# The middle third of the adaLN modulation: from TensorE to row sums on VectorE

## The chip, the cores and the metric

One core of a Trainium2 chip runs the whole program. The metric is the device time of one execution in microseconds; lower is better. TensorE (PE) multiplies matrices, VectorE (DVE), ScalarE (ACT) and GpSimd (POOL) work on rows of 128 partitions, SyncE (SP) here only issues transfers. Every engine takes its own instructions in order; engines wait for one another on semaphores.

## What is computed

Two groups of 128 tokens (context and latent) go through two layers. Each layer begins its modulation from the condition, one row for each group, and uses the same weights for both:

```python
def _modulation(cond, w, b):
    m = jax.nn.silu(cond) @ w + b            # [1, 1024] @ [1024, 6144]
    return jnp.split(m[:, None, :], 6, axis=-1)

sh1, sc1, g1, sh2, sc2, g2 = _modulation(c, p['ada_w'], p['ada_b'])
mix = mixers(_modulate(x, p['norm1'], sh1, sc1), ...)   # three branches: MLA, RG-LRU, differential attention
x = x + g1 * mix
x = x + g2 * _moe(_modulate(x, p['norm2'], sh2, sc2), p)  # top 4 of 32 experts
```

Thirds of the 6144 outputs are made at three times: sh1 and sc1 before the first norm, g1 and sh2 (the middle third) in the middle, sc2 and g2 before the second norm. g1 is first needed when the mixers' output is added to x, sh2 at the second norm. All is float32.

## The kernel before

**Stages of a layer.** The front part: norm, modulation third 0, input projection (units u of `win_mm`), MLA projections, recurrent gates and scans, the merge with its gates, attention in 12 units (8 MLA heads, 4 differential heads), output projection, second norm, router. Then 13 expert passes or more, which stream the expert weights.

**Weights and the ring.** The front's weights stand in DRAM as 32 positions of up to 2 MB (`front`), and go through a ring of 6 slots in SBUF: position p lies in slot p % 6. SyncE issues them strictly in order of position (L416 to L420); each waits until the position 6 places before it has been used (`consumed`, L332). Positions 15 to 18 are the middle third of `ada_w`, 19 the branch-1 output weights, 20 and 21 the gates of branch 0, 23 its output weights, 22 and 24 the gates of branch 2, 25 to 28 the last third of `ada_w`. After position 31 come the first expert weights (L430), each when a slot is free.

**The middle third before.** `ada_products(1, 0)` on TensorE (L545): the SiLU of the condition (`cT`, 128 x 32 columns of which two are used) is the stationary side and the weights stream, 4 positions x 8 = 32 products (64 matmul records). Its output is copied by ScalarE (`modulation`, L1046), transposed back by TensorE (L554), and VectorE adds the bias into `modT` and makes `g1h` = g1/2 (L1201). It stands on TensorE between the eight gate products of branch 1 (`merge(8)`, L675) and the first output product (`merge(1)`, L679). `mod_rdy` 2 is awaited before the transposes of the first attention unit (L684).

**The merge.** A list MERGE of 56 products is worked off in order, its items placed between other work. Product f writes one of two PSUM halves, so it waits until product f - 2 has been evacuated (`merge_evac`, L351): gates by ScalarE (`merge_gates`, a Tanh, L1043), output products by VectorE (`merge`, L1415 to L1443). Products 0 to 7 are gates of branch 1 (positions 13 and 14), then output products and gates alternate from 8 on: 8 is the first output product, 9 the first gate of branch 0 (position 20), 24 the first output product of branch 0.

**Order on the engines around the change.** ScalarE: input projections evacuated up to `win_evac(13)` (L1027), a store, `merge_gates(8)`, `modulation(1, 0)`, then attention. VectorE: norms and rotations of the MLA heads, the scans of both directions (L1357 to L1389), the norms and rotations of the differential heads (L1392 to L1406), two operations on lambda (L1409, L1410), `modulation(1, 1)`, `merge(1)`, then in each attention unit: maxima (L1459), a copy, the probabilities (L1472 or L1480 to L1484, `pn_v`), one or two merge evacuations, and in units 8 to 11 the norm of the head's output (L1497 to L1507). TensorE in a unit: scores, the next unit's transposes, a gate product (two products from unit 8 on), the transposes of the probabilities, an output product, the product with the values.

Of the kernel before, what the change touches and what calls it, by code (L numbers as in the profile page):

```python
# [20 lines left out]
ALU = mybir.AluOpType  # L21
# [3 lines left out]
P = 128  # L25
D = 1024
# [101 lines left out]
    return len(range(s, PRE, RING)) - 1  # L128

def build(nc, x_in, cond_in, consts, vecs, rows, front, lru_gate_w, router_w, exp_w1, exp_b1, exp_w2, exp_b2,
          cache_ckv, cache_krope, cache_dk, cache_dv, y_out, new_ckv, new_krope, new_lru, new_dk, new_dv):
    ctx = ExitStack()
    with ctx:
        def sb(name, shape, dt=F32):
            return ctx.enter_context(nc.sbuf_tensor(name, shape, dt))
# [35 lines left out]
        ring = sb("ring", [P, RING, SLOT])  # L172
        arena = sb("arena", [P, 21344])
        meta = sb("meta", [P, 3], I32)
        both = sb("both", [P, MAX_EXTRA // 2], I32)
        ps = ctx.enter_context(nc.psum_tensor("ps", [P, 8, 512], F32))

        def at(off, *dims):
# [8 lines left out]
            if len(dims) == 4:  # L187
# [101 lines left out]
            [sem(f"{n}{i}") for i in range(2)] for n in ("nrm_mm", "nrm_sqrt", "hraw", "h_dve", "h_act"))  # L289
        ada_mm, ada_sb, ada_tr, prep, mod_rdy = (sem(n) for n in  # L290
                                                 ("ada_mm", "ada_sb", "ada_tr", "prep", "mod_rdy"))
        sp_abs, sp_ln, lam_exp = sem("sp_abs"), sem("sp_ln"), sem("lam_exp")
        win_mm, win_v, win_a = sem("win_mm"), sem("win_evac_v"), sem("win_evac_a")
        mla_n, conv_rdy = sem("mla_norm"), sem("conv_rdy")
# [37 lines left out]
        def consumed(pos):  # L332

            for r in range(3):
                if S_ADA[r] <= pos < S_ADA[r] + 4:
                    return ada_mm, r + 1
            if pos in S_IN:
                return win_mm, 2 * (S_IN.index(pos) + 1)
            if pos in (S_QB, S_KVB):
                return p4_mm, {S_QB: 4, S_KVB: 10}[pos]  # L340
            return f_mm, max(f for f, m in enumerate(MERGE) if merge_slot(*m) == pos) + 1

        def arrived(eng, pos):
# [67 lines left out]
        with nc.Fori(0, L) as l:  # L411
            with nc.Block() as block:
# [120 lines left out]
                def _(pe):  # L533
# [11 lines left out]
                    def ada_products(r, bank):  # L545

                        slots = [arrived(pe, S_ADA[r] + j) for j in range(4)]
                        for k in range(KC):
                            for j in range(4):
                                last = mm(ps[32 * j:32 * j + 32, bank, :], cT[:, k, :],  # L550
                                          slots[j][:, k * 512:(k + 1) * 512], start=k == 0, stop=k == KC - 1)
                        last.then_inc(ada_mm, 1)

                    def ada_transposes(r, bank):  # L554
                        pe.wait_ge(ada_sb, r + 1)
                        for b in range(4):
                            last = tr(ps[:, bank, b * P:(b + 1) * P], msb[r][:, b * P:(b + 1) * P], ident)
                        last.then_inc(ada_tr, 1)
# [115 lines left out]
                    pe.wait_ge(p3_ev, 5)  # L674
                    merge(8)  # L675
                    pe.wait_ge(win_a, 8)
                    ada_products(1, 0)
                    ada_transposes(1, 1)
                    merge(1)  # L679

                    def qk_transposes(u):
                        if u == 0:
                            pe.wait_ge(mod_rdy, 2)  # L684
                            pe.wait_ge(qn_rdy, 2)
# [226 lines left out]
                def _(act):  # L912
# [80 lines left out]

                    act.wait_ge(prep, 2)
                    A(lam[:, 4:6], lam[:, 0:2], ACT.Exp).then_inc(lam_exp, 1)
                    for u in (6, 7):
                        win_evac(u)
                    for v in range(10):
# [26 lines left out]
                    lru_roots(1)  # L1025
                    win_evac(12)
                    win_evac(13)  # L1027
                    act.wait_ge(win_a, 7)
                    store(new_dv, projd[:, 2, 0, :])

# [13 lines left out]
                              scale=0.5).then_inc(f_ac, 1)  # L1044

                    def modulation(r, bank):  # L1046
                        act.wait_ge(ada_mm, r + 1)
                        A(msb[r], ps[:, bank, :], ACT.Copy).then_inc(ada_sb, 1)

                    merge_gates(8)  # L1050
                    modulation(1, 0)
                    act.wait_ge(lru_rdy, 1)
                    store(new_lru, fin[:, :])
                    act.wait_ge(dn_rdy, 3)
# [91 lines left out]
                def _(dve):  # L1146
# [53 lines left out]

                    def modulation(r, bank):  # L1201

                        dve.wait_ge(ada_tr, r + 1)
                        src = ps[:, bank, :].rearrange("p (b j z) -> p j b z", b=4, j=4)[:, :, :, 0:G]
                        dst = modT[:, 16 * r:16 * r + 16, :].rearrange("p (j b) z -> p j b z", j=4)
                        bias = vec[:, V_ADAB + 16 * r:V_ADAB + 16 * r + 16].rearrange("p (j b) -> p j b", j=4)
                        link(V.tensor_tensor(dst, src, bias[:, :, :, None].broadcast_to((P, 4, 4, G)), ALU.add))
                        if r == 1:
                            V.tensor_scalar(g1h[:, :, :], modT[:, 16:24, :], 0.5, None, ALU.mult).then_inc(mod_rdy, 1)
                        else:  # L1210
                            out, sc, nrm = ((A1, 8, V_N1), None, (A2, 32, V_N2))[r]
                            V.scalar_tensor_tensor(out=out[:, :, :], in0=modT[:, sc:sc + 8, :], scalar=1.0,
                                                   in1=vec[:, nrm:nrm + 8][:, :, None].broadcast_to((P, KC, G)),
                                                   op0=ALU.add, op1=ALU.mult).then_inc(mod_rdy, 1)

                    dve.wait_ge(ada_mm, 1)
                    V.tensor_copy(msb[0], ps[:, 0, :]).then_inc(ada_sb, 1)
# [224 lines left out]
                                                                  op0=ALU.mult, op1=ALU.add)  # L1442
                                last.then_inc(f_dv, 1)  # L1443

                    modulation(1, 1)
                    dve.wait_ge(mod_rdy, 2)
                    merge(1)

                    def qk_copy(u):
# [5 lines left out]
                    for u in range(12):  # L1455
# [18 lines left out]
                        else:  # L1474
# [8 lines left out]
                            for n, c in enumerate((slice(0, 128), slice(128, 384))):  # L1483
                                last = V.scalar_tensor_tensor(out=probs[j][:, 0, c], in0=probs[j][:, 1, c],  # L1484
                                                              scalar=nl[:, n:n + 1], in1=probs[j][:, 0, c],
                                                              op0=ALU.mult, op1=ALU.add)
                        last.then_inc(pn_v, 1)
                        if u != 7:
                            merge(1 if u < 7 else 2)
                        if u < 8 and u % 2:  # L1490
# [2 lines left out]
                        if u >= 8:  # L1493
                            dve.wait_ge(pv_mm, u + 1)
                            if u > 8:
                                dve.wait_ge(ot_mm, u - 8)
                            link(V.tensor_copy(on[:, :, :], ps[:, 5, 0:NT].rearrange("p (g n) -> p g n", g=G)))  # L1497
                            for g in range(G):
                                last = V.tensor_tensor_reduce(out=onsq[:, g, :], in0=on[:, g, :],
                                                              in1=on[:, g, :], scale=1.0, scalar=0.0, op0=ALU.mult,  # L1500
                                                              op1=ALU.add, accum_out=ss[:, g:g + 1])
                            link(last)
                            link(V.tensor_scalar(ss[:, 0:2], ss[:, 0:2], 1.0 / DV, EPS, ALU.mult, ALU.add))
                            rsqrt(ss[:, 0:2])
                            for g in range(G):
                                last = V.tensor_scalar(on[:, g, :], on[:, g, :], ss[:, g:g + 1], None, ALU.mult)
                            last.then_inc(on_v, 1)  # L1507
                    merge(8)
                    modulation(2, 1)
                    merge(8)  # L1510
# [293 lines left out]
```

## Time and profile before

| | |
|---|---|
| median of 3 runs | 1724.07 us (1723.03 to 1724.40) |
| the profiled execution | 1722.77 us, its span 1721.1 us |
| TensorE busy | 1529.2 us (89% of the span) |
| VectorE, ScalarE, GpSimd busy | 565.4, 258.1, 3.8 us |
| transfers | 545.86 MB, mean 317 GB/s |
| granted TensorE clock, mean | 0.946 of full |

How the rows are read. A row of the timeline gives the start in us from the span's start, the length in us, the engine, the line, the operation, what it writes <- what it reads, with shapes where the engine has them, and how many instructions are merged into it (x64); in brackets stands how long the engine was idle before it and what ended that.
### The profile page before, as it was taken

The numbers are of one execution on the slowest core, as the hardware profiler recorded it, in microseconds if no ns is written. First come the engines' busy times: TensorE is split into PE (matmuls) and PEld (weight loads), VectorE is DVE, ScalarE is ACT, GpSimd is POOL, SyncE is SP. The second block draws the span as 40 slices with busy tenths as digits, with TensorE's granted clock in tenths as the row PEclk, the third lists the DMA queues.
The fourth block names the chain that finished last, engine by engine and source line by source line (L and its number), as shares of the span: only waits on it lengthen the run. The fifth ranks groups of instructions, "written<-read, shape, count | busy, mean of one in ns | idle before, by whom it ended". The sixth has DMA issues, their size and how long they took to land. (4 is left out here: it accounts for less than half of the span.)

```text
span 1721.1 us, 20139 instructions
## 1 busy us (share of the span) xinstructions
PE 1529.2 (89%) x8000; PEld 891.9 (52%) x8000; DVE 565.4 (33%) x1443; ACT 258.1 (15%) x579; POOL 3.8 (0%) x6
## 2 busy tenths in 40 slices
PE   4999999989889989595969999999897997996868
PEld 2756788764444444242438477878553543442424
DVE  2368236353611121111133862452615121111112
ACT  2034122030000000000030432220200000000001
POOL 0000000000000000000000000000000000000000
PEclk8999999999989999798989999999998999998979
DMA  9653622938999999999895346338489999999991
GB/s 373 260 199 137 267 110 87 390 154 341 419 432 409 411 430 432 430 429 432 345 368 214 150 153 251 147 133 361 176 347 420 430 408 423 430 430 431 431 419 75
DMA packets 48710, 545.86 MB, mean 317 GB/s; under 512 B 12704, under 2 KB 13472, under 8 KB 15584
## 3 DMA queue, kind: packets, MB, share of 16 engines
q1 hardware_dynamic: 39488, 539.95, 75.6%
q10 hardware_dynamic: 9120, 4.53, 1.0%
q8 instruction: 66, 1.08, 0.2%
q14 instruction: 36, 0.29, 0.0%
HBM read 542.06 MB, written 2.40 MB: 316 GB/s over the span
## 5 line engine op out<-in xcount | busy, mean ns | idle before, releaser
L858 PE MATMUL ps<-ring,arena 128*64 128x512 f32 (+2 forms) x1632 | 373.1, 641 | 62.8 <-DMA ring<-exp_w_dram 36.1
L858 PEld LDWEIGHTS ps<-ring,arena 128*64 128x64 f32 (+2 forms) x1632 | 115.5, 133 | 281.7 <-issue 280.2
L878 PE MATMUL ps<-ring,arena 128*32 128x512 f32 (+2 forms) x768 | 199.6, 662 | 28.3 <-DMA arena<-exp_w_dram 16.3
L858 PE MATMUL ps<-arena 128*32 128x512 f32 (+1 forms) x480 | 189.7, 660 | 9.1 <-DMA ring<-exp_w_dram 9.1
L671 PE MATMUL ps<-hT,ring 128*128 128x256 f32 x768 | 171.4, 379 | 0.0
L671 PEld LDWEIGHTS ps<-hT,ring 128*128 128x128 f32 x768 | 144.1, 190 | 19.4 <-issue 1.0
L878 PE MATMUL ps<-arena 128*64 128x512 f32 (+1 forms) x288 | 124.0, 651 | 26.8 <-DMA ring<-exp_w_dram 26.8
L671 PE MATMUL ps<-arena,ring 128*128 128x256 f32 x640 | 144.6, 380 | 2.9 <-ACT arena L1064 1.6
L671 PEld LDWEIGHTS ps<-arena,ring 128*128 128x128 f32 x640 | 118.8, 190 | 19.0 <-issue 2.7
L632 PE MATMUL ps<-ring,hT 128*128 128x512 f32 (+1 forms) x320 | 119.7, 534 | 1.9 <-DVE hT L1227 1.9
L819 PEld LDWEIGHTS ps<-arena 128*128 128x128 f32 x896 | 107.6, 197 | 24.9 <-issue 19.0
L819 PE MATMUL ps<-arena 128*128 128x128 f32 x896 | 114.8, 283 | 3.9 <-DVE arena L1553 3.9
L1126 ACT ACTIVATE arena<-arena 128x512 f32<-128x512 f32 x26 | 16.4, 630 | 668.8 <-DVE arena L1662 668.8
L878 PEld LDWEIGHTS ps<-ring,arena 128*32 128x32 f32 (+2 forms) x768 | 58.6, 136 | 100.8 <-issue 100.8
L1560 DVE TENSOR_TENSOR arena<-arena 128x256 f32<-128x256 f32 x26 | 11.0, 425 | 282.9 <-PE ps L858 282.8
L1674 DVE COPY arena<-ps 128x512 f32<-128x512 f32 x26 | 18.0, 692 | 241.4 <-PE ps L878 241.4
L886 PE MATMUL ps<-arena 128*128 128x256 f32 x416 | 96.5, 385 | 0.0
L886 PEld LDWEIGHTS ps<-arena 128*128 128x128 f32 x416 | 77.1, 190 | 30.1 <-issue 20.6
L632 PEld LDWEIGHTS ps<-ring,hT 128*128 128x128 f32 x320 | 57.4, 190 | 62.7 <-issue 61.5
L1662 DVE TENSOR_SCALAR arena<-ps 128x512 f32<-128x512 f32 x26 | 18.0, 691 | 190.6 <-PE ps L858 190.6
L858 PEld LDWEIGHTS ps<-arena 128*32 128x32 f32 (+1 forms) x480 | 50.3, 134 | 54.3 <-issue 54.3
L878 PEld LDWEIGHTS ps<-arena 128*64 128x64 f32 (+1 forms) x288 | 33.0, 134 | 74.5 <-issue 74.5
(282 smaller groups left out, 1377.7 us busy)
## 6 DMA issues: line engine op xcount, KB each, us to landing
ring<-exp_w_dram SPq DMA_DIRECT2D x148, 2048.0 KB, 18.7
ring<-front_dram SPq DMA_DIRECT2D x58, 2048.0 KB, 8.8
arena<-exp_w_dram SPq DMA_DIRECT2D x47, 2048.0 KB, 19.4
ring<-front_dram SPq DMA_DIRECT2D x2, 1152.0 KB, 16.2
ring<-front_dram SPq DMA_DIRECT2D x2, 1024.0 KB, 18.2
ring<-front_dram SPq DMA_DIRECT2D x2, 640.0 KB, 27.2
xT<-x_in_dram SPq DMA_DIRECT2D x1, 1024.0 KB, 4.9
arena<-lru_gate_w_dram ACTq DMA_DIRECT2D x4, 256.0 KB, 6.4
```

Of the source, the lines that this page charges most:

```text
L632: last = mm(ps[:, bank, 0:w], hT[:, k, half * P:(half + 1) * P], slot[:, k, :], start=k == 0, stop=k == KC - 1)
L671: last = mm(out, slot[:, k, cols], src[:, k, :], start=k == 0, stop=k == nk - 1)
L819: last = mm(ps[:, 2 + k // 4, (k % 4) * P:(k % 4 + 1) * P], X2[:, g, k * P:(k + 1) * P], S_s[:, g, :], start=g == 0, stop=g == 1)
L858: last = mm(ps[c, h, :], xTg[:, 4 * part + k, c], w[i][:, k, h * 512:(h + 1) * 512], start=False, stop=True, skip_group_check=True)
L878: last = mm(ps[c, 2 + h, :], actT[:, f, c], w[i][:, f, h * 512:(h + 1) * 512], start=f == 0, stop=f == 3)
L886: last = mm(ps[:, 4 + k // 2, (k % 2) * NT:(k % 2 + 1) * NT], O_s[:, k * P:(k + 1) * P], SCT[:, :], start=first and k % 2 == 0, stop=True, ...
L1126: A(sig_s, gate_s, ACT.Sigmoid, scale=ALPHA).then_inc(sig_a, 1)
L1560: V.tensor_tensor(SC_s.rearrange("p g (i w) -> p g i w", i=n), S_s.rearrange("p g (i w) -> p g i w", i=n), cwT[:, :, cols][:, :, :, None]. ...
L1662: V.tensor_scalar(gate_s, ps[:, 0, :], LIMIT, None, ALU.min).then_inc(gate_v, 1)
L1674: V.tensor_copy(O_s[:, 512:1024], ps[:, 3, :]).then_inc(o_v, 1)
```

## The change

The weights of the middle third are laid out with the output features on the partitions: a position holds four blocks of 128 features, each with all 1024 inputs in a row. The condition comes a second time as one row of 2 x 1024 numbers and is copied to all 128 partitions (`cB`, 1 MB written, issued by ScalarE). ScalarE makes its Tanh into one scratch tile (`cjunk`), VectorE multiplies, group by group: cB = (tanh(c/2) + 1) * c, twice the SiLU. Then VectorE makes 32 row sums a layer, one for each block and group: 0.5 * sum(weights * cB) straight into `modT`. Four stand before the first merge evacuation, three in each of units 0 to 7 behind the probabilities, four in unit 8. `middle_modulation` adds the bias and makes `g1h` after unit 11. TensorE's products and transposes of this third, ScalarE's copy and the wait for `mod_rdy` 2 on TensorE go. The ring slots of positions 15 to 18 are now freed by every eighth row sum (`ada_v`). The counts of `ada_mm`, `ada_sb` and `ada_tr` are renumbered.

```diff
@@ consumed()
             for r in range(3):
                 if S_ADA[r] <= pos < S_ADA[r] + 4:
-                    return ada_mm, r + 1
+                    return (ada_v, pos - S_ADA[r] + 1) if r == 1 else (ada_mm, r // 2 + 1)
@@ TensorE
                     merge(8)
                     pe.wait_ge(win_a, 8)
-                    ada_products(1, 0)
-                    ada_transposes(1, 1)
                     merge(1)
...
                         if u == 0:
-                            pe.wait_ge(mod_rdy, 2)
                             pe.wait_ge(qn_rdy, 2)
@@ ScalarE
                     A(lam[:, 4:6], lam[:, 0:2], ACT.Exp).then_inc(lam_exp, 1)
+                    act.dma_start(cB[:, :, :].rearrange("p g n -> p (g n)"), cond_rows.broadcast_to((P, G * D))).then_inc(
+                        ld_cb, 16)
...
                     win_evac(12)
                     win_evac(13)
+                    act.wait_ge(ld_cb, 16)
+                    for g in range(G):
+                        if g:
+                            act.wait_ge(cb_prod, g)
+                        A(cjunk[:, :], cB[:, g, :], ACT.Tanh, scale=0.5).then_inc(cb_tanh, 1)
                     act.wait_ge(win_a, 7)
                     store(new_dv, projd[:, 2, 0, :])
...
                     merge_gates(8)
-                    modulation(1, 0)
@@ VectorE
+                    dots = [0]
+
+                    def modulation_dots(n):
+
+                        for _ in range(n):
+                            i, g = dots[0] // G, dots[0] % G
+                            dots[0] += 1
+                            if i % 4 == 0 and g == 0:
+                                arrived(dve, S_ADA[1] + i // 4)
+                            slot = ring[:, (S_ADA[1] + i // 4) % RING, :].rearrange("p (c k) -> p c k", k=D)
+                            last = V.tensor_tensor_reduce(out=cjunk[:, :], in0=slot[:, i % 4, :], in1=cB[:, g, :],
+                                                          scale=0.5, scalar=0.0, op0=ALU.mult, op1=ALU.add,
+                                                          accum_out=modT[:, 16 + i, g:g + 1])
+                            if i % 4 == 3 and g == 1:
+                                last.then_inc(ada_v, 1)
+                                dve.wait_ge(ada_v, i // 4 + 1)
+                            else:
+                                link(last)
+
+                    def middle_modulation():
+
+                        dve.wait_ge(ada_v, 4)
+                        link(V.tensor_tensor(modT[:, 16:32, :], modT[:, 16:32, :],
+                                             vec[:, V_ADAB + 16:V_ADAB + 32][:, :, None].broadcast_to((P, 16, G)),
+                                             ALU.add))
+                        V.tensor_scalar(g1h[:, :, :], modT[:, 16:24, :], 0.5, None, ALU.mult).then_inc(mod_rdy, 1)
...
-                    modulation(1, 1)
-                    dve.wait_ge(mod_rdy, 2)
+                    for g in range(G):
+                        dve.wait_ge(cb_tanh, g + 1)
+                        V.scalar_tensor_tensor(out=cB[:, g, :], in0=cjunk[:, :], scalar=1.0, in1=cB[:, g, :],
+                                               op0=ALU.add, op1=ALU.mult).then_inc(cb_prod, 1)
+                    dve.wait_ge(cb_prod, 2)
+                    modulation_dots(4)
                     merge(1)
...
                         last.then_inc(pn_v, 1)
+                        modulation_dots(3 if u < 8 else 4 if u == 8 else 0)
                         if u != 7:
                             merge(1 if u < 7 else 2)
...
+                    middle_modulation()
+                    dve.wait_ge(mod_rdy, 2)
                     merge(8)
                     modulation(2, 1)
```

## Rows read from the trace of the kernel before

**Rows 1.** The page's busy times, us (share of the span) xinstructions.
```profile
PE 1529.2 (89%) x8000; PEld 891.9 (52%) x8000; DVE 565.4 (33%) x1443; ACT 258.1 (15%) x579; POOL 3.8 (0%) x6
```
**Rows 2.** Timeline of TensorE: gate products, the removed block, what follows; then layer 1.
```profile
153.43 27.79 PE L671 MATMUL ps<-hT,ring 128*128 128x256 f32 x128
181.15 7.07 PE L550 MATMUL ps<-ring,cT 128*32 128x512 f32 x64
...
189.43 1.89 PE L671 MATMUL ps<-arena,ring 128*128 128x256 f32 x8
...
193.67 3.62 PE L671 MATMUL ps<-hT,ring 128*128 128x256 f32 x16
...
1031.82 7.07 PE L550 MATMUL ps<-ring,cT 128*32 128x512 f32 x64
```
**Rows 3.** Windows: the attention units 8 to 11.
```profile
253.00:304.80 51.80, 51.80 (x282) 44.21 (x281) 32.42 (x135) 13.64 (x49) 0.00 (x0) 1.00 0.34 135
```
**Rows 4.** Timeline of SyncE's queue: the first expert weights of layer 0.
```profile
312.66 1.76 SPq L430 DMA_DIRECT2D ring<-exp_w_dram  x3
```
**Rows 5.** Timeline of VectorE: its chain before the removed block; then layer 1.
```profile
155.55 1.22 DVE L1389 TENSOR_TENSOR arena<-arena 128x1024 f32<-128x1024 f32 x1
...
176.33 0.16 DVE L1410 TENSOR_TENSOR lam<-lam,vec 128x1 f32<-128x1 f32 x1
189.70 0.19 DVE L1207 TENSOR_TENSOR modT<-ps,vec 128x32 f32<-128x32 f32 x1 [13.21 <-PE ps L557]
...
1026.99 0.16 DVE L1410 TENSOR_TENSOR lam<-lam,vec 128x1 f32<-128x1 f32 x1
```
**Rows 6.** Timeline of ScalarE: win_evac(13) and the first gate.
```profile
153.63 0.60 ACT L968 ACTIVATE arena<-ps 128x512 f32<-128x512 f32 x1 [2.73 <-PE ps L632]
...
157.08 0.47 ACT L1043 ACTIVATE arena<-ps,bmh 128x256 f32<-128x256 f32 x1 [1.56 <-PE ps L671]
```
**Rows 7.** Timeline of ScalarE: one operation over 2048 and one over 512 elements.
```profile
5.64 1.91 ACT L394 ACTIVATE arena<-xT 128x2048 f32<-128x2048 f32 x1 [3.63 <-DMA xT<-x_in_dram]
...
147.51 0.63 ACT L992 ACTIVATE arena<-arena 128x512 f32<-128x512 f32 x1
```
**Rows 8.** Timeline of TensorE after waits of several lengths; windows behind the first.
```profile
27.26 9.59 PE L550 MATMUL ps<-ring,cT 128*32 128x512 f32 x64 [13.14 <-DMA ring<-front_dram]
...
456.92 7.07 PE L858 MATMUL ps<-ring,arena 128*32 128x512 f32 x64 [3.26 <-DMA ring<-exp_w_dram]
...
1309.39 8.53 PE L858 MATMUL ps<-ring,arena 128*32 128x512 f32 x64 [3.37 <-DMA ring<-exp_w_dram]
...
28.10:30.60 2.50, 2.50 (x16) 0.67 (x12) 2.47 (x6) 1.28 (x2) 0.00 (x0) 0.50 0.99 419
...
32.80:36.80 4.00, 4.00 (x40) 1.09 (x32) 0.40 (x2) 0.00 (x0) 0.00 (x0) 1.00 1.14 323
```
**Rows 9.** One line's instructions: the 20 ring loads of 60 to 330 us.
```profile
DMA to landing us min/median/max: 7.0/7.7/22.2
```
**Rows 10.** Timeline of VectorE: two row sums of squares (L1240, L1244).
```profile
58.00 0.56 DVE L1240 CUSTOM_DVE_ANT_0 arena<-arena 128x384 f32<-128x384 f32 x1
...
58.48 0.42 DVE L1244 CUSTOM_DVE_ANT_0 arena<-arena 128x256 f32<-128x256 f32 x1
```
**Rows 11.** Timeline of VectorE in attention units 1 and 2.
```profile
201.03 0.29 DVE L1459 TENSOR_REDUCE nm<-ps 128x1 f32<-128x128 f32 x1 [1.23 <-PE ps L723]
...
202.84 0.55 DVE L1472 TENSOR_SCALAR arena<-arena,rcp 128x128 f32<-128x128 f32 x2
207.09 0.42 DVE L1426 SCALAR_TENSOR_TENSOR arena<-arena,ps 128x256 f32<-128x256 f32 x1 [3.71 <-PE ps L671]
...
208.74 0.29 DVE L1459 TENSOR_REDUCE nm<-ps 128x1 f32<-128x128 f32 x1 [0.43 <-PE ps L723]
```
**Rows 12.** Timelines of VectorE and TensorE in attention unit 8.
```profile
258.39 0.41 DVE L1431 SCALAR_TENSOR_TENSOR arena<-arena,ps 128x256 f32<-128x256 f32 x1
...
259.98 1.89 PE L671 MATMUL ps<-arena,ring 128*128 128x256 f32 x8
```

More of the change, by code:

```diff
@@ L128, in later_uses, with build @@
     return len(range(s, PRE, RING)) - 1
-def build(nc, x_in, cond_in, consts, vecs, rows, front, lru_gate_w, router_w, exp_w1, exp_b1, exp_w2, exp_b2,
+def build(nc, x_in, cond_in, cond_rows, consts, vecs, rows, front, lru_gate_w, router_w, exp_w1, exp_b1, exp_w2, exp_b2,
           cache_ckv, cache_krope, cache_dk, cache_dv, y_out, new_ckv, new_krope, new_lru, new_dk, new_dv):
@@ L174, in build @@
         meta = sb("meta", [P, 3], I32)
+        cB = sb("cB", [P, G, D])
+        cjunk = sb("cjunk", [P, D])
         both = sb("both", [P, MAX_EXTRA // 2], I32)
@@ L291, in build @@
                                                  ("ada_mm", "ada_sb", "ada_tr", "prep", "mod_rdy"))
+        ld_cb, cb_tanh, cb_prod, ada_v = sem("cond_rows_in"), sem("cond_tanh"), sem("cond_silu"), sem("ada_dve")
         sp_abs, sp_ln, lam_exp = sem("sp_abs"), sem("sp_ln"), sem("lam_exp")
@@ L554, in ada_transposes @@
                     def ada_transposes(r, bank):
-                        pe.wait_ge(ada_sb, r + 1)
+                        pe.wait_ge(ada_sb, r // 2 + 1)
                         for b in range(4):
@@ L1046, in modulation @@
                     def modulation(r, bank):
-                        act.wait_ge(ada_mm, r + 1)
+                        act.wait_ge(ada_mm, r // 2 + 1)
                         A(msb[r], ps[:, bank, :], ACT.Copy).then_inc(ada_sb, 1)
                     merge_gates(8)
-                    modulation(1, 0)
                     act.wait_ge(lru_rdy, 1)
@@ L1201, in modulation @@
                     def modulation(r, bank):
-                        dve.wait_ge(ada_tr, r + 1)
+                        dve.wait_ge(ada_tr, r // 2 + 1)
                         src = ps[:, bank, :].rearrange("p (b j z) -> p j b z", b=4, j=4)[:, :, :, 0:G]
@@ L1207, in modulation @@
                         link(V.tensor_tensor(dst, src, bias[:, :, :, None].broadcast_to((P, 4, 4, G)), ALU.add))
[L1208 to L1214, printed above, removed]
+                        out, sc, nrm = ((A1, 8, V_N1), None, (A2, 32, V_N2))[r]
@@ new lines, in modulation @@
+                        V.scalar_tensor_tensor(out=out[:, :, :], in0=modT[:, sc:sc + 8, :], scalar=1.0,
+                                               in1=vec[:, nrm:nrm + 8][:, :, None].broadcast_to((P, KC, G)),
+                                               op0=ALU.add, op1=ALU.mult).then_inc(mod_rdy, 1)
+                    dots = [0]
[14 more added lines that the diff above has]
+                                link(last)
@@ L1763 @@
         for j in range(4):
-            front[S_ADA[r] + j] = blocks(a["ada_w"], (4 * r + j) * 512, 512)
+            c0 = (4 * r + j) * 512
+            if r == 1:
+                front[S_ADA[r] + j] = a["ada_w"][:, :, c0:c0 + 512].transpose(0, 2, 1).reshape(
+                    L, 4, P, D).transpose(0, 2, 1, 3).reshape(L, P, -1)
+            else:
+                front[S_ADA[r] + j] = blocks(a["ada_w"], c0, 512)
     for p, (c0, n) in zip(S_IN, IN_SLICES):
@@ L1776 @@
         "cond_in": cond.T.reshape(KC, P, G).transpose(1, 0, 2),
-        "consts": constants(np), "vecs": vecs, "rows": rows,
+        "cond_rows": cond.reshape(1, -1), "consts": constants(np), "vecs": vecs, "rows": rows,
         "front": np.concatenate(front, axis=2),
@@ L1789 @@
             "new_dk": (L, P, 512), "new_dv": (L, P, 512)}
-    nc = _bacc.Bacc("TRN2", target_bir_lowering=False, num_devices=1)
+    nc = _bacc.Bacc("TRN2", target_bir_lowering=False, num_devices=1, dynamic_dma_scratch_size=1024)
     given, args = {}, []
```

## The prediction

> **What bounds the kernel now.** I read the page first: TensorE is busy 89% of the span, VectorE 33%, ScalarE 15% [rows 1]. That is a mean over two different halves of each layer (front, then experts), so next I read the timeline by engine around the operations that the change touches, in layer 0. Layer 1 repeats it: there the block that the change removes begins 1031.82 - 1026.99 = 4.83 us after VectorE's last operation of its chain, in layer 0 181.15 - 176.33 = 4.82 us [rows 2, 5]. Between 153.43 and 181.15 us TensorE runs the eight gate products of branch 1 with no gap (3.46 us each), then the 64 matmuls of the second modulation (7.07 us), a short wait, four transposes and the first product of the merge at 189.43 [rows 2]. The attention that follows is TensorE's as well: 51.80 of 51.80 us busy in its second part [rows 3]. So TensorE is the bound of the front part, and what is taken from or added to its chain counts in full. The front's end sets the expert part too: the transfers of expert weights are issued only from 312.66 us on, since each waits for a ring slot that the front's last products free [rows 4]. Nothing there can run ahead, so a front that is late by x makes the layer late by x.
>
> **Removed from TensorE.** The block of ada_products(1) and ada_transposes(1) with its copy on ScalarE and its two operations on VectorE runs from 181.15 to 189.43 us: -8.28 us per layer [rows 2]. VectorE then was idle 13.21 us before it had this to do [rows 5], so its own removal is worth nothing.
>
> **Added on ScalarE, and its wait.** This is where I expect the time to go. The new order on ScalarE is win_evac(13), Tanh of group 0, a wait for cb_prod 1, Tanh of group 1, and only then merge_gates(8). cb_prod 1 comes from VectorE's product for group 0, which the change puts where modulation(1,1) stood: behind the scans, the four squares, the norms and the rotations of the differential heads and behind L1410. In the trace that chain is dense from 154 us to L1410 at 176.33 + 0.16 = 176.49 us [rows 5], while ScalarE is free from 154.2 us and makes its first gate at 157.08 [rows 6]. So queued behind ScalarE's wait are all eight gates, and TensorE waits for them: there are two PSUM halves for the merge, so product 2 needs gate 0 evacuated. It began at 153.43 + 2 x 3.455 = 160.34 us. Now: VectorE's product over 128x1024 takes 1.22 us (as L1389 [rows 5]), 176.53 to 177.78. ScalarE's Tanh over 1024 elements is in no row; 512 take 0.63 and 2048 take 1.91 [rows 7], so 0.83 ns an element in between and 1.06 us, to 178.87; the gate of 0.47 us overlaps it by 0.1 and ends at 179.25. TensorE goes on at 179.3: a stall of **18.96 us** per layer. The first Tanh (154.2 to 156.6 with the table load of 1.28 us that moves there) is hidden, as is the product of group 1 (to 180.2) and the first four sums (to 185.4), since VectorE's next duty, the first merge, is not due before TensorE has made six more gates (20.8 us).
>
> After long waits TensorE is slow: the 64 matmuls of L550 take 9.59 us after 13.14 us idle [rows 8] and 7.07 us where they follow other work [rows 2]; behind the wait the granted clock is 0.50, the lower level of 1.2 GHz, and from 32.8 us on 1.00 [rows 8]. I add +2.2 us (bounds 1.5, as 64 matmuls of the experts with 8.53 us for 7.07 [rows 8], and 2.5).
>
> **The slot of position 20.** Its ring slot (2) is freed by gate product 7, the last before the removed block, and it holds the first gates of branch 0, product 9. Before, 181.15 to 193.67 = 12.5 us lay between; without the block it is 193.67 - 189.43 = 4.24 us [rows 2]. A 2 MB load takes 7.0 us at least from issue to landing and 7.7 in the median [rows 9]; alone on the queue I take 7.0. So the removed block was the cover of this load, and **+2.8 us** come back (up to 3.5). The Trainium skill has a price for it ("DMA: Bandwidth & Descriptors", section on what a DMA costs: about 2.0 us plus the bytes by 436 GB/s), which would be 6.8 us and a stall of 2.6 us; the row is used.
>
> **The sums of products on VectorE.** 32 per layer, over 1024 elements, each linked to the next. The same operation over 384 elements takes 0.56 us, over 256 0.42 [rows 10], so 1.09 ns an element; for 1024 that is 1.26 us, and I take 1.27 with the link (1.2 to 1.5). In units 0 to 7 three of them, 3.81 us, go between the probabilities (203.39) and the merge's operation at 207.09, where VectorE is idle 3.71 us [rows 11]: 0.1 us late. The merge's result is needed by TensorE only in the next unit and the next maximum is due at 208.74 [rows 11]; with 0.44 and 0.42 us for the two operations in between, up to (208.74 - 203.39 - 0.86) / 3 = 1.50 us each are hidden. Cost 0. Unit 8 has four, 5.08 us, and no such gap: there the merge follows the probabilities at once at 258.39, and TensorE starts product 26 at 259.98, which needs product 24 evacuated [rows 12]. Now the sums run 258.39 to 263.47, the two operations of the evacuation to 264.33, and product 26 starts at 264.38: **+4.4 us** (4.1 to 5.3). VectorE's long chain after it (norm of the head) shifts equally, and later units have no idle time that could give it back [rows 3].
>
> **Positions 21 to 24** are freed by sums 8, 16, 24 and 32 instead of all at 188 us. 21 and 22 have several units to land. A unit takes 208.74 - 201.03 = 7.71 us [rows 11]; 23 is issued with the second sum of unit 6 at 203.39 + 5 x 7.71 + 2.5 = 244.4 us, lands by 252.1 and is needed in unit 8, which begins at 253: hidden by a microsecond or two. 24 is issued in unit 8 with 25 to 27 queued behind it on SyncE (some 20 us of transfer); it is needed in unit 10 and they after unit 11, some 45 us on: nothing. The load of the condition (1 MB, written to all partitions) goes out on ScalarE's queue near 43 us and is wanted at 154: nothing; the ring's loads that it shares the engines with have 9 us of reserve. middle_modulation is 0.5 us on VectorE while TensorE makes the third modulation: hidden.
>
> **Clock after the two short waits.** After waits of 3.26 and 3.37 us the next 64 matmuls took 7.07 and 8.53 us [rows 8]: 0 to 1.5 us more. I take 0.8 for each of the two, **+1.6 us**. The Trainium skill ("TensorE: Matmul & The Clock Gate", section "HAM oscillation") says that a wait for data of this size puts the array back to the lower clock each time. By it each would cost the full 2.2 us and the kernel 5.6 us more in all.
>
> **Sum.** Per layer -8.28 + 18.96 + 2.2 + 2.8 + 4.4 + 1.6 = +21.7 us, two layers +43.4. On the profiled execution's 1722.77 us (span 1721.1 and 1.67 around it) that is 1766.2; the runs' median of 1724.07 lies 1.3 above it. I predict 1766.5 us.
>
> **Rivals.**
> (A) ScalarE is not held, because cb_prod 1 can come before VectorE's chain is over, so not slower: -8.28 + 2.8 + 4.4 + 1.6 = +0.5 per layer, 1724 us. For it: the operation needs nothing of that chain. Against it: it stands behind it in the one order of VectorE, which shows no gap in the chain. It decides as soon as cb_prod 1 comes before 157 us. Chance 0.03.
> (B) Only the hold counts; position 20 lands in time and the sums of unit 8 delay nothing: 2 x (18.96 + 2.2 - 8.28) = +25.8, 1748.6 us. For it: loads were never waited for in this stage. Against it: 4.24 against 7.0 us, and 5.08 us of sums ahead of an evacuation with 0.7 us of slack. Chance 0.12 (for either of the two vanishing, 1752 to 1760).
> (C) The sums are slower than their small relatives. From 1.57 us on, VectorE's unit (3.2 us + three sums) is longer than TensorE's 7.71 and becomes the bound: at 1.7 us 8 x 0.39 less the 1.4 us of slack = 1.7 us per layer and 1.7 more in unit 8: 1773 us. Chance 0.08.
> (D) The lower clock after each wait, as the rule above has it: 1772 us. Chance 0.12.
> (E) The change does nothing of this, because the compiler or the queues order the operations otherwise: 1724. Below 0.02, no row speaks for it.
> My own case has the rest, 0.64.
>
> **Range.** Its low end is all clock costs at 0 and 1.2 us sums (+17.6 per layer, 1758), and case B with one term gone at 1752; the high end is 2.5, 3.5, 4.4 and 3.0 (+24.1 per layer, 1771), and C to 1773. I give 1753 to 1775. A measurement of this kernel tells about 0.2% (3.4 us) from no change. Slower 0.96, within 0.02, faster 0.02.
>
> **What will show it.** In the changed kernel: ScalarE idle some 20 us between two Tanh of 128x1024, released by VectorE; TensorE idle 19 us at the third gate product with ScalarE as the releaser, and the lower clock behind it; 2.8 us before product 9, released by a DMA; 32 sums near 1.26 us a layer; 4.4 us in unit 8 before product 26, released by VectorE. No gap in units 1 to 7. What would prove me wrong: the first gate at 157 us as before (A), or gaps in every unit (C).

## The result, and the profile after

The changed kernel takes 1775.16 us in the median of 4 runs (1774.53 to 1777.90) against 1724.24 us before: a ratio of 1.0302, 95% interval 1.0288 to 1.0317. It is slower by 51 us. I had forecast +43 (1766.5 us) and a range up to 1775.0; the direction and the three places were right, and the size fell just outside.

The profiled execution has a span of 1773.9 us. First the busy times of its page, to be read against [rows 1]: TensorE has 136 records fewer (2 x 68) and is yet busy 5.4 us longer, since other products became slower; VectorE has 82 us more, of which 78.3 us are the 64 row sums (1223 ns each).

```profile
PE 1534.6 (87%) x7864; PEld 898.5 (51%) x7864; DVE 647.4 (36%) x1575; ACT 260.8 (15%) x581; POOL 3.8 (0%) x6
```
```profile
L1229 DVE CUSTOM_DVE_ANT_0 cjunk<-ring,cB 128x1024 f32<-128x1024 f32 x64 | 78.3, 1223 | 1.6
```

The places are in TensorE's timeline of layer 0, which answers to [rows 2, 12]. Brackets: idle time before the row and what ended it.

```profile
152.40 7.07 PE L674 MATMUL ps<-hT,ring 128*128 128x256 f32 x32
178.21 23.95 PE L674 MATMUL ps<-hT,ring 128*128 128x256 f32 x96 [18.74 <-ACT arena L1050]
201.99 1.89 PE L674 MATMUL ps<-arena,ring 128*128 128x256 f32 x8
...
209.84 6.22 PE L674 MATMUL ps<-hT,ring 128*128 128x256 f32 x16 [3.46 <-DMA ring<-front_dram]
...
278.43 0.49 PE L742 MATMUL ps<-cst,arena 128*128 128x128 f32 x3
283.15 3.68 PE L674 MATMUL ps<-arena,ring 128*128 128x256 f32 x8 [4.24 <-DVE arena L1463]
```

Three waits stand there that before had none: 18.74 us before gate product 2, released by ScalarE; 3.46 us before product 9, released by a transfer; 4.24 us before product 26, released by VectorE. Behind each the products are longer: six gates in 23.95 us where eight took 27.79, so 3.1 us too long; product 9 in 6.22 for 3.62; product 26 in 3.68 for 1.89.

What holds ScalarE is in its timeline, which answers to [rows 6]: two Tanh of 1024 elements, with 21.17 us between them that end with VectorE's product (L1477), and only then the gates.

```profile
154.51 1.06 ACT L1034 ACTIVATE cjunk<-cB 128x1024 f32<-128x1024 f32 x1
176.73 1.06 ACT L1034 ACTIVATE cjunk<-cB 128x1024 f32<-128x1024 f32 x1 [21.17 <-DVE cB L1477]
...
177.70 0.82 ACT L1050 ACTIVATE arena<-ps,bmh 128x256 f32<-128x256 f32 x2
```

VectorE in unit 8: the last of the four sums, then at once the evacuation for which product 26 waits. Before, that evacuation began with the end of the probabilities [rows 12].

```profile
277.16 1.22 DVE L1229 CUSTOM_DVE_ANT_0 cjunk<-ring,cB 128x1024 f32<-128x1024 f32 x1
...
280.95 1.22 DVE L1229 CUSTOM_DVE_ANT_0 cjunk<-ring,cB 128x1024 f32<-128x1024 f32 x1
282.11 0.08 DVE L1229 DVE_READ_ACCUMULATOR2_ANT modT<- 128x1 f32 x1
282.22 0.42 DVE L1461 SCALAR_TENSOR_TENSOR arena<-arena,ps 128x256 f32<-128x256 f32 x1
```

Last, the windows of the changed kernel around the three waits; the third figure from the right is the granted clock.

```profile
171.10:178.20 7.10, 0.00 (x0) 0.00 (x0) 5.70 (x11) 1.47 (x3) 0.00 (x0) 0.50 0.08 30
...
181.00:184.00 3.00, 3.00 (x9) 2.37 (x8) 2.93 (x5) 0.00 (x0) 0.00 (x0) 0.50 0.00 0
184.00:187.00 3.00, 3.00 (x15) 2.64 (x14) 0.11 (x2) 0.48 (x1) 0.00 (x0) 0.96 0.00 0
206.40:209.80 3.40, 0.00 (x0) 0.00 (x0) 2.81 (x8) 1.18 (x5) 0.00 (x0) 0.75 0.92 360
...
212.00:214.00 2.00, 2.00 (x6) 1.55 (x6) 0.00 (x0) 0.00 (x0) 0.00 (x0) 0.50 0.00 0
...
278.90:283.10 4.20, 0.02 (x1) 0.00 (x0) 4.06 (x8) 0.00 (x0) 0.00 (x0) 1.00 0.00 0
283.10:285.00 1.90, 1.84 (x5) 1.49 (x6) 0.00 (x0) 0.85 (x2) 0.00 (x0) 0.53 0.93 276
```

Behind all three the clock is at its lower level, 0.50 (1.2 GHz), behind the short ones as well. At the first two it fell while TensorE was still idle (0.50 and 0.75 in the idle stretches); at the third the idle stretch still has 1.00 and the products behind it 0.53.

**The account.** From the first gate product to the router's products (L786) layer 0 takes 388.03 - 152.40 = 235.63 us; before it was 363.06 - 153.43 = 209.63. That is +26.0, layer 1 has +26.15. The parts for layer 0: 18.74 + 3.1 - 8.28 = +13.6 up to the first output product; 3.46 + 2.60 and some 0.15 = +6.2 at product 9; 4.24 + 1.79 and some 0.15 = +6.2 in unit 8 (in these rows a product begins 0.15 us before the end of the one before it where no wait parts them, and a wait takes that away too). The remaining 52.8 - 52.15 = 0.6 us of the span lie in the start and the experts.

### The profile page after: what moved, and what is told of

Read it like the earlier page. It is cut to its first block and busy times, and to the rows that moved or that the text cites. A ratio compares the mean times of both kernels' runs of the same rounds, so it can differ in the third digit from the quotient of the medians.

```text
span 1773.9 us, 20021 instructions
## 1 busy us (share of the span) xinstructions
PE 1534.6 (87%) x7864; PEld 898.5 (51%) x7864; DVE 647.4 (36%) x1575; ACT 260.8 (15%) x581; POOL 3.8 (0%) x6
## 5 line engine op out<-in xcount | busy, mean ns | idle before, releaser
L674 PE MATMUL ps<-hT,ring 128*128 128x256 f32 x768 | 182.9, 396 | 44.8 <-ACT arena L1050 37.5
L674 PEld LDWEIGHTS ps<-hT,ring 128*128 128x128 f32 x768 | 151.6, 200 | 68.5 <-ACT arena L1050 38.3
L1229 DVE CUSTOM_DVE_ANT_0 cjunk<-ring,cB 128x1024 f32<-128x1024 f32 x64 | 78.3, 1223 | 1.6
```

Of the source, the lines that this page charges most:

```text
L674: last = mm(out, slot[:, k, cols], src[:, k, :], start=k == 0, stop=k == nk - 1)
L1229: last = V.tensor_tensor_reduce(out=cjunk[:, :], in0=slot[:, i % 4, :], in1=cB[:, g, :], scale=0.5, scalar=0.0, op0=ALU.mult, op1=ALU.add, ...
```

## The experiments

**1. ScalarE not held.** The Tanh of group 1 writes a free part of the arena instead of the scratch tile, and waits for the scans only.

```diff
-                        if g:
-                            act.wait_ge(cb_prod, g)
-                        A(cjunk[:, :], cB[:, g, :], ACT.Tanh, scale=0.5).then_inc(cb_tanh, 1)
+                        if g:
+                            act.wait_ge(lru_fr, 2)
+                        A((cjunk[:, :], at(E0, D))[g], cB[:, g, :], ACT.Tanh, scale=0.5).then_inc(cb_tanh, 1)
...
+                    act.wait_ge(cb_prod, 2)
                     qk_copy(0)
```

> The changed kernel, but the Tanh of group 1 goes into a free part of the arena, so ScalarE doesn't wait for VectorE's chain and the gates go on at once. Theory (the hold costs its wait of 18.74 us and 3.15 us of lower clock behind it, per layer, and the other terms stay): 1775.2 - 2 x 21.9 = 1731.4 us, with TensorE still waiting 3.5 to 3.8 us for position 20 and 4.2 us in unit 8. Rival (the clock price behind the short waits comes from the long one before them): these 64 and 32 matmuls run at full clock, 2 x 2.6 us less, about 1726 us. Rival (the four sums, now due right when the first merge is, delay the first scores): 1 to 2 us more per layer, 1734.

Measured: 1731.78 us, ratio 1.0058 (1.0037 to 1.0080) to the kernel before. That is the time of my theory within 0.4 us: the hold with the lower clock behind it is 43 of the 51 us. The timeline of TensorE in layer 0 (first three rows) and layer 1 (last row) has the eight gates in one piece again, and the other two waits:

```profile
152.98 27.79 PE L674 MATMUL ps<-hT,ring 128*128 128x256 f32 x128
...
184.48 0.49 PE L722 MATMUL ps<-arena 96*128 96x128 f32 x2 [1.44 <-DVE arena L1487]
...
188.41 5.31 PE L674 MATMUL ps<-hT,ring 128*128 128x256 f32 x16 [2.46 <-DMA ring<-front_dram]
...
1043.60 6.08 PE L674 MATMUL ps<-hT,ring 128*128 128x256 f32 x16 [3.91 <-DMA ring<-front_dram]
```

The four sums delay the first scores by 0.9 us (1.44 for 0.52). In layer 0 the wait for position 20 is shorter by as much; in layer 1 it is 3.91 us all the same. Product 9 is slow in both (5.31 and 6.08 us) though no long wait precedes it, so the first rival falls.

**2. Eight sums first.** The four sums of unit 8 move before the attention.

```diff
-                    modulation_dots(4)
+                    modulation_dots(8)
...
-                        modulation_dots(3 if u < 8 else 4 if u == 8 else 0)
+                        modulation_dots(3 if u < 8 else 0)
```

> The changed kernel with the four row sums of unit 8 made before the attention (eight there, none in unit 8). Theory (unit 8 costs 4.24 us of wait and 1.8 us of lower clock per layer): 1775.2 - 2 x 6.0 = 1763.2 us, no wait of TensorE for VectorE in unit 8, and the eight sums hidden in VectorE's 19.9 us of idle time. Rival (the wait only moves to the next evacuation, since VectorE's norm of the head follows at once): under 2 us gained, 1773.

Measured: 1763.53 us, ratio 1.0237 (1.0220 to 1.0254), and no wait for VectorE in unit 8. Four sums at the wrong place cost 11.6 us in the two layers, a little more than their own 2 x 5.08 us, since the lower clock comes on top of the wait. Product 26 of layer 0 follows without a wait, at its old length:

```profile
280.93 0.49 PE L742 MATMUL ps<-cst,arena 128*128 128x128 f32 x3
281.26 1.89 PE L674 MATMUL ps<-arena,ring 128*128 128x256 f32 x8
```

**3. The hold alone, in the kernel before.**

```diff
+                    V.tensor_copy(krs[:, 3:4], lam[:, 7:8]).then_inc(hold, 1)     # VectorE, behind L1410
...
+                    act.wait_ge(hold, 1)                                          # ScalarE
                     merge_gates(8)
```

> The kernel before, with nothing but ScalarE's wait: the eight gates wait for a small VectorE operation behind L1410. Theory (the hold alone costs 18.7 us of wait and 3.15 us of lower clock): 1724.2 + 2 x 21.9 = 1768.0 us, and no wait for position 20, which the second modulation still covers. Rival (the clock price is that of my forecast, 2.2 us): 1766. Rival (part of the hold is absorbed, since VectorE and the loads run ahead meanwhile): under 1760.

Measured: 1763.04 us, ratio 1.0230 (1.0213 to 1.0247), 5 us under what I wrote. The wait is 16.73 us, not 18.74: this kernel has neither VectorE's product (1.23 us) nor the second Tanh (1.06 us) between the chain and the gates, which I had forgotten in the expectation. With 2.1 to 2.5 us of slow products behind it, 2 x 19.0 = 38 us on 1723.5 gives 1761.5. The waits of layer 0 and 1:

```profile
179.42 22.93 PE L672 MATMUL ps<-hT,ring 128*128 128x256 f32 x96 [16.73 <-ACT arena L1044]
...
1049.12 23.27 PE L672 MATMUL ps<-hT,ring 128*128 128x256 f32 x96 [16.73 <-ACT arena L1044]
```

The six gates take 22.93 and 23.27 us for 20.8, so behind a wait of 16.7 us the lower clock costs 2.1 and 2.4 us. On this term the first rival was right, and not the 3.15 us that I had taken over from the changed kernel: the price of a long wait is not one number. No wait for position 20 follows: the second modulation, still there, covers it.

**4. The block left out of the kernel before.** The products, copy and transposes of the middle third are left out, and the bias alone stands in modT, so this kernel does less than the reference; the weights are still loaded, and TensorE still waits for their arrival.

```diff
-                    merge(8)
+                    merge(7)
+                    for j in range(4):
+                        arrived(pe, S_ADA[1] + j)
+                    merge(1)
                     pe.wait_ge(win_a, 8)
-                    ada_products(1, 0)
-                    ada_transposes(1, 1)
```

> The kernel before without the middle third: its products, copy and transposes are left out and modT's third is the bias alone; its weights are still loaded and awaited. Theory (the block also covered the load of position 20): per layer -8.28 + 3.5 of wait + 2.5 of lower clock = -2.3, 1719.6 us, with a wait for a DMA before product 9. Rival (the block is worth its whole 8.28 us): 1707.7 us and no wait.

Measured: 1718.99 us, ratio 0.9977 (0.9965 to 0.9990), as the theory had it to 0.6 us. (The expert part of layer 1 gets other data here, so tenths are not to be read from it.) Even with nothing in its place the removed block is worth 4.5 us, not 16.6, since the load that it covered comes to light at once:

```profile
186.04 0.46 PE L722 MATMUL ps<-arena 96*128 96x128 f32 x2 [0.52 <-DVE arena L1452]
...
191.32 6.47 PE L671 MATMUL ps<-hT,ring 128*128 128x256 f32 x16 [3.84 <-DMA ring<-front_dram]
```

**5. Both mends, 1 and 2, together.**

> Both edits of the first two experiments: ScalarE not held, and eight sums before the attention, none in unit 8. Theory: the gain of unit 8 stays (2 x 6.0 us from 1731.8), but VectorE's idle time before the first merge is gone too, since TensorE is there 22 us earlier: chain to 175.5, two products and eight sums to 188.1, so the first scores come 6 us late; 3.5 of these lie under the wait for position 20, 2.5 don't: 1731.8 - 2 x 3.5 = 1724.8 us. Rival (sums before the attention are free): 1719.8.

Measured: 1725.99 us, ratio 1.0012 (1.0001 to 1.0023). The theory is off by 1.2 us. TensorE waits 6.50 us for the first transposes' copy, and behind it the granted clock is low again, 0.50 (the window below): product 9 takes 5.48 us though it has no wait of its own.

```profile
189.98 0.80 PE L722 MATMUL ps<-arena 96*128 96x128 f32 x2 [6.50 <-DVE arena L1487]
...
192.49 5.48 PE L674 MATMUL ps<-hT,ring 128*128 128x256 f32 x16
```
```profile
192.00:194.00 2.00, 2.00 (x8) 1.71 (x7) 1.54 (x6) 1.18 (x5) 0.00 (x0) 0.50 0.98 418
```

So sums before the attention are free only as long as TensorE is late itself.

**6. Early sums.** Both Tanh and both products near 70 to 81 us, four sums between the scan directions, four behind L1410, none in unit 8.

```diff
+                    act.wait_ge(ld_cb, 16)                 # ScalarE, ahead of win_evac(6)
+                    for g in range(G):
+                        A((cjunk[:, :], at(0, D))[g], cB[:, g, :], ACT.Tanh, scale=0.5).then_inc(cb_tanh, 1)
...
                         last.then_inc(lru_fr, 1)           # VectorE, in the loop over scan directions
+                        if d == 0:
+                            modulation_dots(4)
...
-                        modulation_dots(3 if u < 8 else 4 if u == 8 else 0)
+                        modulation_dots(3 if u < 8 else 0)
```

> The Tanh and the products with the condition made near 70 to 81 us, where ScalarE and VectorE are idle; four sums between the two scan directions, in VectorE's idle 6.2 us, four behind L1410, three in each of units 0 to 7, none in unit 8. Theory: all that is left of the change's costs is the wait for position 20 with its lower clock, per layer -8.28 + 3.6 + 2.5 = -2.2 us: 1719.1 us. Rival (a sum delays the recurrent chain or the ScalarE work behind it): a gap of TensorE elsewhere, 1722 or more.

Measured: 1718.42 us, ratio 0.9978 (0.9969 to 0.9988). The same time as without the whole computation (experiment 4): the 64 sums are hidden, and what is left is position 20. The timelines say it more sharply than the times: from gates to router this kernel takes 206.04 and 206.61 us in the two layers against 209.64 before, and 208.12 and 208.20 in experiment 4, and the 2 us between the two kernels in layer 0 are a shorter wait (3.16 us) with a cheaper low clock (1.5 us) before product 9:

```profile
190.84 5.08 PE L674 MATMUL ps<-hT,ring 128*128 128x256 f32 x16 [3.16 <-DMA ring<-front_dram]
```

So the front saves 3.6 and 3.0 us a layer where the theory had 2.2; that the whole time still came out as written is in part luck: 2.2 us are lost ahead of the first gate product (at 155.66 us for 153.43) and 2.4 us between the last router and the end (509.8 us for 507.4).

**7 and 8. Two or three output products ahead of the first gate of branch 0.** On top of 6 the merge list is shifted, so that more of TensorE's work lies between the issue of position 20 and its first use.

```diff
-for _b, _next in ((1, 0), (0, 2)):
-    for _ch in range(KC):
-        MERGE += [("proj", _b, _ch), ("gate", _next, _ch)]
+LEAD = 3                                                  # 2 in experiment 7
+MERGE += [("proj", 1, _ch) for _ch in range(LEAD)]
+for _ch in range(KC):
+    MERGE += [("gate", 0, _ch)] + ([("proj", 1, _ch + LEAD)] if _ch + LEAD < KC else [])
+for _ch in range(KC):
+    MERGE += [("proj", 0, _ch), ("gate", 2, _ch)]
```

> As the kernel with early sums, and two output products of branch 1 instead of one before the first gate of branch 0 (the merge list is shifted by one; unit 6 has no output product left). It gives the load of position 20 1.73 us more cover. Theory: the wait falls from 3.6 to 1.9 us, and behind so short a wait no lower clock; unit 6 without its output product costs 0.6 us, as unit 7 does: per layer -8.28 + 1.9 + 0.6 = -5.8, 1712 us. Rival (the lower clock comes after every wait): 1716.

Measured: 1715.93 us, ratio 0.9959 (0.9945 to 0.9973). The rival is right: the waits are 3.05 us in layer 0 and 1.86 us in layer 1, and behind even the shorter one the product takes 5.17 us for 3.62.

```profile
1037.87 5.17 PE L677 MATMUL ps<-hT,ring 128*128 128x256 f32 x16 [1.86 <-DMA ring<-front_dram]
```

> As before with three output products ahead: cover 4.24 + 3.46 = 7.7 us against a load of 7.2 to 7.8. Theory: no wait, no lower clock, 1.2 us for units 5 and 6 without their output product: per layer -8.28 + 0.1 + 1.2 = -7.0, 1709.5 us. Rival (the three evacuations on VectorE delay the first scores): 1 us more per layer.

Measured: 1712.14 us, ratio 0.9937 (0.9921 to 0.9954): 0.6% faster than the kernel before, beyond the interval, and the best version. No wait for a transfer is left in this stage; the rows of layer 0 show the gate of unit 0 at almost its full rate and a 0.62 us wait in one of the units without its output product.

```profile
188.72 3.69 PE L677 MATMUL ps<-hT,ring 128*128 128x256 f32 x16
...
231.91 0.43 PE L759 MATMUL ps<-arena 128*64 128x128 f32 x2 [0.62 <-ACT arena L1092]
```

From gates to router it saves 6.90 and 6.94 us in the two layers, 13.8 as expected; the span is only 10.7 shorter. In the last experts 3.4 us are lost again (510.8 us from the router's products to the end, 507.4 before), and 0.3 us are gained elsewhere. In the other kernels of this study with the same experts that stretch is 505.8 to 510.3 us, so one profiled execution doesn't tell whether the new order has a part in it. Why it differs is open.

**9. The waits filled.** The disputed term is what comes behind a wait. Here TensorE makes products that nobody reads instead of idling, in the changed kernel.

```diff
+                            if f == 2:
+                                pe.wait_ge(lg_ev, 16)
+                                fill(84)
+                            if f == 9:
+                                fill(14)
+                            if f == 26:
+                                pe.wait_ge(om_ev, 4)
+                                fill(18)
                             if f >= 2:
                                 merge_evac(pe, f)
```

> The changed kernel with every new wait of TensorE filled by products nobody reads: 84 of 128x256 before gate product 2 (18.1 of the 18.7 us), 14 before product 9 (3.0 of 3.5), 18 before product 26 (3.9 of 4.2). The waits themselves stay as long; only the idling goes. Theory (behind each wait the next products are slow because TensorE idled, 3.15 + 2.5 + 1.75 us per layer): the six gates take 20.8 us, product 9 3.6, product 26 1.9, and the kernel 1775.2 - 2 x 7.4 = 1760.4 us. Rival (the products behind the waits are slow for another reason, data or PSUM late): 1775 as before.

Measured: 1805.06 us, ratio 1.0473 (1.0456 to 1.0491). I had counted matmul records for products: the fills took twice the time and overran the waits. The experiment says little by its time, but the six gates behind took 20.88 us. So it was made again:

> As the kernel with the filled waits, with half the products: a float32 product of 128x256 is two matmul records and takes 0.432 us, so 84, 14 and 18 of them took 36.3, 6.0 and 7.8 us and overran the waits. 42, 7 and 9 take 18.1, 3.0 and 3.9 us and fit. Theory (the lower clock comes from the idling): the products behind the waits at full clock, 1775.2 - 2 x 7.4 = 1760.4 us. Rival (they are slow for another reason): 1775.

Measured: 1756.94 us, ratio 1.0213 (1.0185 to 1.0241); on the 1724.24 of the changed kernel's comparison that ratio is 1760.9 us, as the theory has it. The waits end at the same events, and the products behind them are back at their full rate:

```profile
160.00 18.29 PE L653 MATMUL ps<-hT,cst 128*128 128x256 f32 x84
178.88 20.99 PE L686 MATMUL ps<-hT,ring 128*128 128x256 f32 x96 [0.59 <-ACT arena L1062]
...
203.94 3.19 PE L653 MATMUL ps<-hT,cst 128*128 128x256 f32 x14
207.38 3.69 PE L686 MATMUL ps<-hT,ring 128*128 128x256 f32 x16 [0.26 <-DMA ring<-front_dram]
...
273.77 4.05 PE L653 MATMUL ps<-hT,cst 128*128 128x256 f32 x18
278.18 1.99 PE L686 MATMUL ps<-arena,ring 128*128 128x256 f32 x8 [0.35 <-DVE arena L1475]
```
```profile
206.00:212.00 6.00, 5.74 (x29) 4.75 (x28) 3.55 (x6) 0.85 (x2) 0.00 (x0) 1.00 0.22 85
```

The same stretch that had a granted clock of 0.50 to 0.75 has 1.00. More work on TensorE made the kernel some 15 us faster (10 to 19 us by the interval of the filled kernel): the slow products come from the idling, and not from late data or PSUM, whose waits are still there.

**10. The new order alone, in the kernel before.** The merge list of experiment 8, with the second modulation where it was.

> The kernel before with the new order of the merge alone: three output products of branch 1 ahead of the first gate of branch 0, none in units 5 and 6. Theory: nothing to win there, since the second modulation covers the load; 0.6 us more in each of units 5 and 6: 1723 + 2.5 = 1725.5 us. Then the gain of the best version comes from the block that left TensorE. Rival (the order itself is better): under 1720.

Measured: 1723.99 us, ratio 1.0005 (0.9995 to 1.0015). It gives nothing by itself; the 11 us of the best version are the removed block, once its cover is replaced.

## Why the prediction was right or wrong

**The direction and the places were right.** All three waits are where the sum had them, with the releasers that it named.

**The block removed, -8.28 us:** right. Experiment 4 shows it with its counterpart.

**ScalarE's hold, 18.96 us:** right, 18.74 in both layers. The Tanh that no row showed took 1.06 us, as interpolated.

**Position 20, 2.8 us:** right in kind, a bit small: 3.46 and 3.84. I took the fastest landing of [rows 9] for a load that has the queue to itself; the median, 7.7 us, would have given 3.5. In the kernel before this load did land in 7.0 us. In the changed one it took 7.4 and 7.8 us in the two layers, and within the same 4 us ScalarE issued two stores (256 KB and 4 KB), so it was not alone; no run took them away. The 6.8 us by the Trainium skill ("DMA: Bandwidth & Descriptors", section "Anatomy of one DMA — SWDGE (gpsimd) path") are worked from a fit that the page gives for transfers issued by GpSimd, while SyncE issues this one; that estimate is 0.6 us below the 7.4 us of layer 0.

**Row sums:** right. 1.22 us each and 1.27 from one to the next; hidden in units 0 to 7, where TensorE has no new wait, and 4.24 us in unit 8 for a forecast 4.4.

**The expert part:** right here. What the front lost came out at the end, to 0.6 us. In experiments 6 and 8 the last experts alone took 2.4 and 3.4 us longer than before, with no change to them.

**The lower clock behind the waits was the step that failed.** It had 2.2 us behind the long wait and 0.8 behind each short one, 3.8 us per layer. Measured are 3.1, 2.6 and 1.8 in layer 0, together 7.5, and 3.1, 2.4 and 1.7 in layer 1, together 7.3. The difference of 3.7 and 3.5 us is 7.2 us of the 9.4 us by which the forecast of the span was short (52.8 us for 43.4); the rest is position 20 (0.7 and 1.0 us) and 0.6 us outside the front parts. The 0.8 was a mean of two rows from expert passes, one of them without any loss [rows 8]. But the kernel before also had a 3.56 us wait in the same front part, before the router's products, whose windows I had read and not used. And my range let each short wait cost 1.5 us at most, the larger of two rows, when such waits cost up to 3.1 us in the other runs (5.08 to 6.75 us for product 9 behind them). The rule of the Trainium skill that I put down as rival D ("TensorE: Matmul & The Clock Gate", section "HAM oscillation") was the better guide: each short wait put the array back to its lower clock. By it the sum was 1772 us, and with the median landing 1773.5. The runs agree with it on all waits of 1.86 us and more in the front part.

**The range** then missed by 0.2 us. Its high end took each unknown near the larger of the values seen, but the clock terms had been seen only two or three times, and all three lie outside together, since one cause sets them. Case D with the late landing, 1773.5 us, was still inside it. With the 2.5 us of the slowest row seen [rows 8] for each of the three waits the sum is -8.28 + 18.96 + 3 x 2.5 + 3.5 + 4.4 = 26.1 us per layer, 1774.9 us: a range that took D seriously had to reach beyond that. Giving D a chance of 0.12 was the other mistake.

**Two slips in the rivals** changed nothing in the forecast. In C the unit of VectorE is given as 3.2 us and three sums, but its threshold of 1.57 us and its 0.39 us per unit belong to 3.0 us; with 3.2 they are 1.50 and 0.59. And A and E, both of them "no change", have 0.03 and up to 0.02, while the chances by class leave 0.02 for it.

## What to carry to other kernels

When an engine gets a wait in the middle of its order, list what stands behind it and who waits for that: a scratch tile shared by two operations cost 43 of the 51 us here, and a second place for its data took it away. A block that is taken from the bounding engine was also cover for a transfer; before counting its time as gained, look up which load is issued just ahead of it and needed just behind it. Every new wait of TensorE is to be priced with its duration and 1.5 to 3 us more for the lower clock behind it (1.5 to 3.1 us behind the new waits of 1.86 to 18.7 us here); only a run tells how much of it comes.

## What I had not expected of the hardware

How short a wait is enough for the lower clock. In the front part of these kernels, waits of 1.86, 2.46, 3.05, 3.16, 3.46, 3.84, 4.24 and 6.50 us were all followed by products at a granted clock near 0.50, and product 9, where it stood behind one, took 5.1 to 6.8 us for 3.62. Before each of them stand attention steps with small matmuls. In an expert pass of the kernel before, a wait of 3.26 us had no such effect [rows 8].

A still shorter wait goes both ways in one and the same place. Behind the router each kernel has a wait of 1.34 us before the same 32 records. They take 5.3 to 5.5 us in most of the traces, and 3.84 us in layer 0 of experiments 1, 6, 7, 10 and 11 and in both layers of experiment 9. Here are the kernel before and experiment 6, each with its window:

```profile
372.91 5.47 PE L819 MATMUL ps<-arena 128*128 128x128 f32 x32 [1.34 <-DVE arena L1553]
...
375.00:378.40 3.40, 3.40 (x22) 3.28 (x22) 0.00 (x0) 0.00 (x0) 0.00 (x0) 0.69 0.00 0
```
```profile
372.31 3.84 PE L819 MATMUL ps<-arena 128*128 128x128 f32 x32 [1.34 <-DVE arena L1590]
...
372.40:376.10 3.70, 3.70 (x33) 3.58 (x33) 0.64 (x5) 0.00 (x0) 0.00 (x0) 1.00 0.02 4
```

So the length of a wait alone doesn't decide it. What makes the difference is open; no run here tells it.
